# Sample attention as one pipeline of sequence pairs, and an earlier first tile of the projection

## The reference

```python
z = h @ w_in;  qa, ka, va, qb, kb, vb, fa = split(z)        # after RMS norm; 8 heads of 64 in each group
# group A, forgetting attention over 16 pages of 128 cached keys per sequence
s = q @ k_page.T * scale + cn[..., None] + r_page            # r: summed forget values behind each key
p = exp(s - max);  acc = p @ v_page;  oa = acc / p.sum()     # new keys included
# group B, dilated window of 2048 cached keys per sequence, dilations 1, 4 and 16
# for every (w, d): keys back by 0, d, ..., w; the three results merged by their softmax denominators
x = x + concat(oa, ob) @ w_o;  x = x + relu(rms(x) @ w_up)**2 @ w_down
```

## Time and profile before

| | us |
|---|---|
| median of 3 runs | 4157.27 (4154.04 to 4157.55) |
| the profiled execution | 4158.81, its span 4157.3 |
| projection, until its first matmul of a product | 0 to 34.85 |
| samples with pages (sfox) | 1718.7 to 2124 |
| samples with windows (sdil) | 2124 to 2380.4 |
| output projection and MLP | 2380.4 to 4157.3 |
| mean granted clock of TensorE over the span (1 is full) | 0.952 |

### The profile page before, as it was taken

How to read it: one execution, slowest core, us unless ns; L and a number is a source line. 1 busy time by engine, 2 the same in 40 slices (tenths; PEclk the granted TensorE clock), 3 DMA queues, 4 the chain that set the end, 5 groups by cost and what they waited for, 6 DMA issues and landing times. The chain is left out here.

```text
span 4157.3 us, 50242 instructions
## 1 busy us (share of the span) xinstructions
PE 3792.6 (91%) x18252; PEld 2891.4 (70%) x18252; DVE 1502.4 (36%) x3122; ACT 1035.1 (25%) x1481; POOL 682.2 (16%) x641
## 2 busy tenths in 40 slices
PE   6999995999977999888878698999999889999999
PEld 6987784555535777544434376888887778989898
DVE  2223332554535555222112233343443334343333
ACT  3322221344431333211111132121121321111111
POOL 1223465320000111131100011000000110010000
PEclk9999998999987999899989799999999899999999
DMA  5556666655636564486445222111111311111111
GB/s 179 188 169 207 212 214 218 150 156 134 172 115 147 170 182 127 133 269 179 129 166 204 74 100 71 41 59 42 40 61 51 129 51 41 51 50 40 40 40 56
DMA packets 293751, 504.85 MB, mean 121 GB/s; under 512 B 79113, under 2 KB 202634, under 8 KB 281162
## 3 DMA queue, kind: packets, MB, share of 16 engines
q1 hardware_dynamic: 276770, 401.37, 31.4%
q10 hardware_dynamic: 2464, 67.37, 4.4%
q0 software_dynamic: 14368, 34.10, 2.8%
HBM read 406.94 MB, written 163.45 MB: 137 GB/s over the span
## 5 line engine op out<-in xcount | busy, mean ns | idle before, releaser
L2312 DVE TENSOR_TENSOR fin_x<-mlp_y,fin_x 128x512 f32<-128x512 f32 x544 | 350.2, 686 | 741.5 <-PE mlp_y L2355 741.5
L2332 PE MATMUL mlp_u<-fin_h_hi,mlp_w_hi 128*128 128x512 f32 (+2 forms) x1280 | 451.6, 353 | 28.6 <-DVE mlp_w_lo L2288 28.6
L2333 PE MATMUL mlp_u<-fin_h_lo,mlp_w_hi 128*128 128x512 f32 (+2 forms) x1280 | 451.2, 353 | 0.0
L2334 PE MATMUL mlp_u<-fin_h_hi,mlp_w_lo 128*128 128x512 f32 (+2 forms) x1280 | 451.2, 352 | 0.0
L2353 PE MATMUL mlp_y<-mlp_w_hi,mlp_u_hi 128*128 128x512 f32 x1088 | 423.9, 390 | 1.2 <-DVE fin_x L2312 1.2
L2354 PE MATMUL mlp_y<-mlp_w_lo,mlp_u_hi 128*128 128x512 f32 x1088 | 424.3, 390 | 0.0
L2355 PE MATMUL mlp_y<-mlp_w_hi,mlp_u_lo 128*128 128x512 f32 x1088 | 423.9, 390 | 0.0
L2272 POOL TENSOR_TENSOR mlp_u<-mlp_r 128x1024 f32<-128x1024 f32 (+2 forms) x80 | 131.7, 1647 | 1328.4 <-ACT mlp_r L2213 1328.4
L661 PE MATMUL proj_z<-proj_w_hi,proj_x_hi 128*128 128x512 f32 (+1 forms) x816 | 310.6, 381 | 41.4 <-POOL proj_x_lo L458 24.4
L663 PE MATMUL proj_z<-proj_w_hi,proj_x_lo 128*128 128x512 f32 (+1 forms) x816 | 304.4, 373 | 0.0
L662 PE MATMUL proj_z<-proj_w_lo,proj_x_hi 128*128 128x512 f32 (+1 forms) x816 | 304.0, 373 | 0.0
(11 more groups left out here) (255 smaller groups left out, 6363.8 us busy)
## 6 DMA issues: line engine op xcount, KB each, us to landing
sfox_k_in<-in_cache_k SPq DMA_DIRECT2D x128, 256.0 KB, 3.0
sfox_v_in<-in_cache_v POOLq DMA_DIRECT2D x128, 256.0 KB, 3.2
mlp_w_raw<-in_w_up SPq DMA_DIRECT2D x64, 512.0 KB, 3.8
mlp_w_raw<-in_w_down SPq DMA_DIRECT2D x64, 512.0 KB, 4.5
out_new_win_k<-in_win_k ACTq DMA_DIRECT2D x8, 4080.0 KB
out_new_win_v<-in_win_v ACTq DMA_DIRECT2D x8, 4080.0 KB
proj_x_hi<-scratch_xt SPq DMA_DIRECT2D x34, 512.0 KB, 6.4
proj_x_lo<-scratch_xt SPq DMA_DIRECT2D x34, 512.0 KB, 6.3
```

Source lines behind the costliest of these rows:

```text
L2312: dve.tensor_tensor(part, y_ps[(tiles * par + t) % 2][0:rows, q * D_G:(q + 1) * D_G], part, ALU.add).then_inc(y_added, 1)
L2332: pe.matmul(out, hi, h_hi[:, k, c0:c0 + n], start=(k == 0), stop=False)
L2333: pe.matmul(out, hi, h_lo[:, k, c0:c0 + n], start=False, stop=False)
L2334: mm = pe.matmul(out, lo, h_hi[:, k, c0:c0 + n], start=False, stop=(k == KC - 1))
```

## The change

In the projection, x's first tile and four weight pieces come first, then the second tile, then the other four pieces; two more slots for raw weights and a buffer for the squares are added, and g_attn has a semaphore of its own.

sample_attend is replaced by attend_samples: one stage for windows (four pairs, first) and pages (four pairs, after them), as a written-out sequence of 33 slots with no loop. A slot turns the keys of one group (4 or 2 tiles, both sequences), multiplies the scores of the group before, and turns and multiplies the exponentials of a group of the pair before. Its turns are dealt into three batches: one ahead of the scores, one after them, one after the values. Three banks t_ps take the turns; the keys are emptied by ScalarE and VectorE in turn, exponentials by ScalarE. Scores and values go through the two sequences alternately, matmul by matmul. k_in and v_in hold three groups; all values are loaded by GpSimd. unreached is added by a matmul with an identity in bfloat16; the pages' summed forget values are computed once for all sequences (slots 3 to 5), written to DRAM by 16 DMAs of ScalarE's queue, read back (r_all), and added by one matmul for a group with a selecting matrix (pick). The maximum, the exponential and the product with reach go by groups.

In the code below, lines of functions that are new throughout keep the mark that the diff gives them; removed lines are shown for the projection alone.

```diff
+            for k in range(1, 4):
+                load_w(0, k)
             load_x(1, 0, 1)
-            for k in range(W_SLOTS):
+            for k in range(4, KC):
+                if k >= W_SLOTS:
+                    sp.wait_ge(w_split, k - W_SLOTS + 1)
                 load_w(0, k)
-            sp.dma_start(g_attn[:, :], dram["g_attn"]).then_inc(consts, 16)
             sp.dma_start(b_f[:, :], dram["b_f"].partition_broadcast(P)).then_inc(consts, 16)
             for n, name in enumerate(("g_qa", "g_ka", "g_qb", "g_kb")):
...
+            hi_x(0, 0)
+            for k in range(4):
                 hi_w(0, k)
-            act.wait_ge(w_split, KC)
-            hi_x(0, 0)
             hi_x(0, 1)
+            for k in range(4, KC):
+                hi_w(0, k)
             scale(0, 0, 0)
             hi_x(0, 2)
...
             for j in range(2):
                 gain_x(0, j)
                 mean_x(0, j)
+                for k in range(4 * j, 4 * j + 4):
+                    lo_w(0, k)
+            dve.wait_ge(consts, 16 * 7)
             for i in range(0, PAIRS - 1):
                 for j in range(2):
...
+KV_SLOTS = 3
+T_BANKS = 3
...
+DIL_TILES = [4, 4, 2]
+FOX_TILES = [4] * (PAST // PAGE // 4)
+STAGES = [(True, i) for i in range(PAIRS_S)] + [(False, i) for i in range(PAIRS_S)]
...
+GROUP_BASE = [sum(len(x) for x in GROUPS[:n]) for n in range(len(STAGES) + 1)]
+N_GROUPS = GROUP_BASE[-1]
+SLOTS = N_GROUPS + 1 + len(GROUPS[-1])
+LF_SLOT, R_SLOT = 3, 5
...
+def values_at(slot):
+    for n in range(len(STAGES)):
+        q = slot - GROUP_BASE[n + 1] - 1
+        if 0 <= q < len(GROUPS[n]):
+            return GROUP_BASE[n] + q
+    return None
+def turns_at(slot):
+    first, rest = [], []
+    v = values_at(slot)
+    if v is not None:
+        n, q = group_at(v)
+        first.append(("p", v, 0, 0))
+        if q == len(GROUPS[n]) - 1:
+            first.append(("w", n, 0, 0))
+    if slot < N_GROUPS:
+        n, g = group_at(slot)
+        if g == 0:
+            first.append(("n", n, 0, 0))
+        rest = [("k", slot, s2, t) for s2 in range(2) for t in range(GROUPS[n][g])]
+    if slot in (LF_SLOT, R_SLOT):
+        rest = [("l" if slot == LF_SLOT else "r", 0, k, 0) for k in range(2)] + rest
+    a = max(0, min(3 - len(first), len(rest)))
+    b = (len(rest) - a + 1) // 2
+    return [first + rest[:a], rest[a:a + b], rest[a + b:]]
...
+            for G in range(N_GROUPS):
+                if G >= KV_SLOTS:
+                    old = G - KV_SLOTS
+                    sp.wait_ge(turned, NUMBER[("k", old, 1, tiles_of(old) - 1)] + 1)
                 for s2 in range(2):
+                    load_kv(sp, G, s2, k_in, k_loaded[G % KV_SLOTS][s2], "win_k", "cache_k")
...
+            def load_v(G):
+                if G >= KV_SLOTS:
+                    pool.wait_ge(pv, G - KV_SLOTS + 1)
+                if G == 2:
+                    pool.wait_ge(mask_set, 1)
+                for s2 in range(2):
+                    load_kv(pool, G, s2, v_in, v_loaded[G % KV_SLOTS][s2], "win_v", "cache_v")
...
+            def exponentials(n):
+                dilated, _i = STAGES[n]
+                act.wait_ge(bounded, n + 1)
+                bias = nm[:, n % 2:n % 2 + 1]
+                for g, tiles in enumerate(GROUPS[n]):
+                    cols = slice(4 * P * g, 4 * P * g + tiles * P)
+                    if dilated:
+                        act.activation(p_sb[:, cols], s_ps[:, cols], ACT.Exp, bias=bias).then_inc(exped, 1)
                     else:
+                        act.activation(p_sb[:, cols], s_ps[:, cols], ACT.Exp, bias=bias,
+                                       accum_out=sums[:, n % 2, g:g + 1]).then_inc(exped, 1)
...
+            for slot in range(SLOTS):
+                a, b, d = turns_at(slot)
+                for x in a:
+                    empty(x)
+                for n in scored_stage(slot):
+                    exponentials(n)
+                for x in b:
+                    empty(x)
+                for x in d:
+                    empty(x)
...
+                if slot == R_SLOT + 1:
+                    wait_emptied(act, NUMBER[("r", 0, 1, 0)])
+                    for half, tile in ((0, r_hi[:, :, :].bitcast(F32)), (1, r_lo)):
+                        for b in range(DEC_BATCH):
+                            act.dma_start(dram["r_rows"][half, b * HEADS:(b + 1) * HEADS, :]
+                                          .rearrange("h (t p) -> t h p", p=P),
+                                          tile[16 * b:16 * (b + 1), :, :]).then_inc(r_sent, 16)
+                if slot == R_SLOT + 2:
+                    act.wait_ge(r_sent, 16 * 2 * DEC_BATCH)
+                    act.dma_start(r_all[:, :].bitcast(F32), dram["r_rows"].rearrange("a b k -> (a b) k"))\
...
+            def weigh(n):
+                dilated, _i = STAGES[n]
+                NG = len(GROUPS[n])
+                for g in range(NG + 1):
+                    dve.wait_ge(exped, maxima(n) + g + 1)
+                    if not dilated:
+                        continue
+                    cols = slice(4 * P * g, 4 * P * g + (GROUPS[n][g] if g < NG else 0) * P)
+                    part = p_sb[:, cols] if g < NG else p_new[:, :]
+                    times = reach[:, cols] if g < NG else reach[:, 10 * P:10 * P + DEC_SEQ]
+                    dve.scalar_tensor_tensor(part, part, 1.0, times, ALU.mult, ALU.mult,
+                                             accum_out=sums[:, n % 2, g:g + 1]).then_inc(weighed, 1)
                 if dilated:
...
+            def turn(x):
+                e = NUMBER[x]
+                what, G, s2, t = x
+                out = t_ps[e % T_BANKS]
+                wait_emptied(pe, e - T_BANKS)
+                if what == "k":
+                    if t == 0:
+                        pe.wait_ge(k_loaded[G % KV_SLOTS][s2], arrived(G))
+                    for j in range(4):
+                        mm = pe.transpose(out[:, j * P:(j + 1) * P],
+                                          k_in[:, G % KV_SLOTS, s2, t, j * P:(j + 1) * P], c["ident"][:, :])
+                elif what == "p":
+                    n, q = group_at(G)
+                    if STAGES[n][0]:
+                        pe.wait_ge(weighed, maxima(n) + q + 1)
+                    else:
+                        pe.wait_ge(exped, maxima(n) + q + 1)
+                    for k in range(tiles_of(G)):
+                        a = 4 * P * q + k * P
+                        mm = pe.transpose(out[:, k * P:(k + 1) * P], p_sb[:, a:a + P], c["ident"][:, :])
+                elif what == "w":
+                    if STAGES[G][0]:
+                        pe.wait_ge(weighed, maxima(G + 1))
+                    else:
+                        pe.wait_ge(exped, maxima(G + 1))
+                    mm = pe.transpose(out[0:DEC_SEQ, 0:P], p_new[:, :], c["ident"][:, :])
...
+            def scores(G):
+                n, g = group_at(G)
+                dilated, i = STAGES[n]
+                tiles = tiles_of(G)
+                w = tiles * P
+                out = s_ps[:, 4 * P * g:4 * P * g + w]
+                if n >= 1 and g < len(GROUPS[n - 1]):
+                    pe.wait_ge(exped, maxima(n - 1) + g + 1)
...
+                    pe.matmul(out, ident_bf[:, :], unreached[:, 4 * P * g:4 * P * g + w], start=True, stop=False)
+                else:
+                    pe.wait_ge(pick_set, 1)
+                    pe.wait_ge(r_loaded, 16)
+                    pe.matmul(out, pick[:, i, :], r_all[:, 4 * P * g:4 * P * g + w], start=True, stop=False)
+                wait_emptied(pe, NUMBER[("k", G, 1, tiles - 1)])
+                wait_emptied(pe, NUMBER[("k", G, 1, tiles - 2)])
                 for j in range(4):
...
+                    for s2 in range(2):
+                        mm = pe.matmul(s_ps[half(s2), 4 * P * g:4 * P * g + w],
+                                       q_bd[:, n % 2, s2, j * SEQROWS:(j + 1) * SEQROWS], kT[:, s2, G % 2, j, 0:w],
+                                       start=False, stop=(j == 3))
+                mm.then_inc(scored, 1)
...
+            def products(G):
+                n, q = group_at(G)
+                last = q == len(GROUPS[n]) - 1
+                tiles = tiles_of(G)
+                for s2 in range(2):
+                    pe.wait_ge(v_loaded[G % KV_SLOTS][s2], arrived(G))
+                wait_emptied(pe, NUMBER[("p", G, 0, 0)])
+                if q == 0 and n > 0:
+                    pe.wait_ge(owned, n)
+                for k in range(tiles):
+                    for s2 in range(2):
+                        mm = pe.matmul(o_ps[half(s2), :], pT[:, G % 2, k * P + s2 * SEQROWS:k * P + (s2 + 1) * SEQROWS],
+                                       v_in[:, G % KV_SLOTS, s2, k, :], start=(q == 0 and k == 0), stop=False)
+                if last:
+                    wait_emptied(pe, NUMBER[("w", n, 0, 0)])
+                    pe.wait_ge(vn_loaded, 16 * (n + 1))
+                    for s2 in range(2):
```

(31 more changed lines are left out.)

728 lines of the change are left out of this document (352 added, 376 removed).

## The result

The changed kernel takes **3888.8 us** (median of 4 runs, 3884.8 to 3891.0) where the kernel before took 4156.1 (4154.0 to 4157.6): a ratio of **0.9356** (95% interval 0.9340 to 0.9372). The forecast was 3908, with 3865 to 3985 as its range. The profiled execution took 3887.9 us with a span of 3886.4, so 270.9 us of span are gone. From the first load of the sample stage on SyncE to the first load of the join stage it is 397.8 us (1712.1 to 2110.0) where it was 656.8 (1723.6 to 2380.4): 258.9 of the 270.9 us went there. The projection and what follows it end 11.5 us earlier; behind the sample stage nothing moved (1776.4 us after 1776.9).

What follows compares the result with a forecast made beforehand. TensorE was taken as the bound, busy 91% of the span. From a span of 4157.3, 15 us for the projection and 236 for the sample stage were subtracted: 3906.3, plus 1.5 beyond the span, 3908; range 3865 to 3985.

Steps and rivals of the forecast that it cites:

- no overlap: Sample stage: instructions alternating on both column halves run one by one, 7.0 us a four-tile batch; +178 us, 4086; chance 0.04.
- strict order: Sample stage: a half's first instruction can't pass the other half's second, one step more a batch; +28, 3936; chance 0.07.
- low clock: TensorE's clock stays at its lower level through the sample stage, doubling its terms; +379 us, 4287; chance 0.04.
- The hand-overs: Sample stage: ScalarE and VectorE empty banks no faster than before, turns cost 0.67; +35, 3943; chance 0.13 together with transfers.
- A turned tile: Sample stage: turning one tile on TensorE takes 0.52 us, bounds 0.47 and 0.67, as three banks no longer set the pace.
- The change of form: Sample stage: TensorE's switch between turns and products costs 0.1 us each, four in a slot.
- The small batches n and w: Sample stage: scores of the new keys (n) and batch w together take 1.6 us a pair with windows, 1.9 with pages.
- The holes: Pair's end: TensorE's fourth turn waits for copies queued behind exponentials, 3.4 us with pages, 2.0 with windows; weighing adds 1.4.
- The terms that occur once: Sample stage: start 18, forget turns and sums 6, DRAM way 6, small sums 1, low clock 6, last slots 4, end 6; together 47.
- better than 3865: Sample stage: turns at 0.47 (-12), exponentials hidden (-22), no low clock (-6); chance 0.07.
- The projection: Projection's start: x goes before the weight splits, first matmul about 15.4, first tile done earlier; 15 us saved, bounds 8 and 19.
- (c): Sample stage: the part of the gain from making the forget sums once; 34.5 us by busy times, not undone alone.

Runs made afterwards that it cites:

- values in every slot: Changed kernel with the products of the values ahead of the second batch of turns in all slots, not behind it: 3864.2 us, ratio 0.9307.

## Why the prediction was right, and where it was off

**The mechanism held.** Scores and values at 3.6 us a batch were measured at 3.58 and 3.59. The rival "no overlap" is out by this row, and the rival "strict order" too: it wanted 4.0. The Trainium skill, page "TensorE: Matmul & The Clock Gate", Part 3 (Packing small matmuls), calls matmuls strictly first in, first out in start and end. The kernel with one half after the other speaks against it: eight instructions of one half 0.43 us apart, with the other half's first no earlier than their last, would end at 15 x 0.43 + 0.16 = 6.6 us, and the row has 5.42, as after 12 steps; and four instructions of each half, one half after the other, took 1.94 us, as after 4 steps, where that order gives 7 x 0.43 + 0.16 = 3.2. The "low clock" rival is out with 0.97 in the stage's body.

**The hand-overs.** The claim that a third bank takes the copies off the path was right, and two banks show its worth: 42 to 51 us, where that rival put 35. Transfers were hidden as predicted: 303 GB/s against the 295 needed, and no wait for them between the first slots and the last values.

**The terms that were mis-sized.** The stage was put at 426 us from the last store of the stage ahead and took 402.7, so 23 us too long. The projection gained less than forecast, so the two errors work against each other in the 3908:
- A turned tile was taken at 0.52 between bounds of 0.47 and 0.67. Nine take 4.18 us, 0.46 to 0.47 each: the lower bound. 234 turns times 0.055 are 13 us.
- The change of form, 0.1 us at four places in a slot and 11 us in all, should not have stood in the sum. Where values follow scores directly (values in every slot), the next batch begins after 3.48 us, and before a turn after 3.58; that tenth is already in the price of a batch, so it was counted twice.
- The small batches n and w, 1.6 and 1.9 a pair, measured about 1.1; the pick 0.41 where 0.3 was taken. These cancel in part.
- The holes were right in place and close in size: 3.11 for 3.4 with pages, 1.60 for 2.0 with windows, 1.48 for 1.4 before the turn of weights. But the sum has one with pages too many: the last pair's exponentials find no keys left to turn, so there are three and not four. Pairs with windows take 35.3 us (1825.94 to 1861.26, from one batch n to the next) for 38.1, with pages and a hole 54.3 (1958.76 to 2013.08) for 56.7.
- The terms that occur once were 47; 402.7 - 4 x 35.3 - 4 x 54.3 leaves 44.3 (about 48 if only three holes are taken off). Inside it two are off: the last four slots, put at 4, lose 7.2 us in waits alone (0.89, 0.78, 0.78 and 4.78 for the last values to arrive) and two of their batches run 1.7 us longer each, at a clock of 0.68 and 0.67; the transfers of the forget rows, put at 6, cost 4.68 of waiting and 2.5 of lower clock. What the others of that sum took by themselves is not shown.
- One sum doesn't come out: the case "better than 3865" takes 12, 22 and 6 us off 3908, which is 3868.

**The projection.** 15 us were forecast. The kernel with this part alone gained 14.5 in time; the profiled execution of the changed kernel shows 11.5, and other executions of the same code up to 18.1. That the 14.5 are so near is in part chance, for the start itself gave less. From the third x tile's turn on, tiles follow each other every 12.2 us in both kernels, and that turn came here (before, then after):

```profile
52.73 1.03 PE L636 MATMUL proj_t<-all_ident,proj_x_in 128*128 128x128 f32 x8
```

```profile
43.44 1.03 PE L641 MATMUL proj_t<-all_ident,proj_x_in 128*128 128x128 f32 x8
```

That is 9.3 us, and up to 11.4 in other executions of the new code (its turn comes at 41.37 to 43.44); what the sample stage's start shows on top arises behind the first tiles, and no run shows why. The details were off: the first product starts at 17.1 instead of 15.4, and the first tile is done, so that ScalarE scales it, at 39.45 instead of 33.5 (48.74 before). The overlooked cause is that the first of VectorE's splits beside each of GpSimd's two subtractions takes 2.54 us and not 1.22; taking GpSimd away gives back 1.3 us at the first product and 2.4 us at the second stretch. And the lower clock behind the hole, put at 1 us, cost about 2.5: 18 matmuls from 31.02 to 36.35, 0.29 us apart and then 0.16.

**What the gain is not.** The prediction gave no share to the overlap of pairs by itself. As built its worth is small, about 19 us of 259, for the reason that the prediction named as a hole: ScalarE's queue order. With the values ahead of the second batch in every slot, the stage is 23.3 us shorter still.

What stays open: why executions of the same code reach the sample stage up to 6.6 us apart, and how much (c) is worth by itself. The parts that were undone or read from rows come to 77 (order), 49 (both sequences in one batch), 51 (third bank), 19 (overlap) and 34.5 (forget sums, by busy time), together 230 of the 259 us; the rest is not divided, and the parts need not add.

## What to carry to other kernels

Pair off narrow matmuls so that consecutive ones use different column halves, and look at the order inside a batch before building a larger pipeline: here swapping two loops, in the scores and in the values, was worth 77 us, about four times what the overlap of pairs was as first built. When stages are overlapped, read which in-order queue carries both the long operation and the small copies that the bottleneck waits for, and put work that needs none of these copies right behind the point where the long operation starts. When a batch's price is taken from start to next start, its hand-over is already in it.

## What the runs showed of the hardware that was not expected

- VectorE's subtraction of two SBUF tensors of 128x1032 takes 1.22 us alone and up to 2.54 us while GpSimd's subtraction (2.36 us) is under way, which itself is not slowed. The Trainium skill, page "SBUF — State Buffer", section "SBUF: two separate sides", says that a VectorE operation with two SBUF inputs and a GpSimd operation that reads SBUF exclude each other for a whole instruction; by that rule the first split, begun at 14.44, would end 1.22 us after GpSimd's end at 15.90, at 17.1; it took 2.54 us, to 16.98, so the trace agrees within 0.14 us.
- Sixteen instructions on two column halves take 3.65, 5.42 or (as two batches of eight) 7.3 us by their order: counted in steps of 0.43 us, instructions of the second half begin some four steps before the first half's are through. With only four instructions of each half the order made no difference (1.94 us).
- A hole of 3.1 us on TensorE cost 1.3 to 1.5 us more in the changed kernel, where the batch behind it ran partly at the lower clock (values 4.9 to 5.2 us in place of 3.65, granted clock 0.50 from 2023.20 to 2026.00). But it doesn't always: in the kernel with the forget rows sent by SyncE, three holes of 3.11 us were followed once by values of 6.15 us (granted clock 0.50 from 1953.80 to 1958.00) and twice by batches at full pace (values of 3.65 us from 2008.98 on, clock 1.00). Which of the two follows, no run here settles.
